# RWKV-7 products in one written order, with the memory projection's ten tiles computed whole at nine places of it

## The reference, cut to what matters

```
def step(s, inp):                                   # RWKV-7, one token, 8 heads of 64
    r_t, w_t, k_t, v_t, kk_t, a_t = inp
    sa = einsum('bhvk,bhk->bhv', s, -kk_t)
    s = s * w_t + sa[..., None] * (kk_t * a_t) + v_t[..., None] * k_t
    return s, einsum('bhvk,bhk->bhv', s, r_t)
s_final, ys = lax.scan(step, s0, xs)
m = mean(y, axis=-1); var = mean(square(y - m), axis=-1)
y = (y - m) * rsqrt(var + GN_EPS) * ln_w + ln_b
out = (y + bonus) * g

mk, mv = split(rmsnorm(mem, g_mem) @ w_mem_kv, 2)   # (256, 1024) each, used by the cross-attention
```

## Time and profile before

| | us |
|---|---|
| median of 3 runs (1435.22 to 1437.1) | 1437.06 |
| the profiled execution's own time | 1435.98 |
| its span | 1434.2 |
| PE busy in it | 1367.2 |
| RWKV jobs, from the fillers of the first to the start of `w_out` | 182.7 to 325.6 |
| experts | from 495 |

### The profile page before, as it was taken

The page is one execution under the profiler, slowest core; times in us unless marked ns, Lnnn a source line. Parts: engine busy times, 40 slices in busy tenths (PEclk is TensorE's granted clock), DMA queues, the critical chain, the costliest instruction groups (busy, mean ns, idle before and its releaser), DMA issues.

```text
span 1434.2 us, 21169 instructions
## 1 busy us (share of the span) xinstructions
PE 1367.2 (95%) x8649; PEld 689.7 (48%) x8649; DVE 440.5 (31%) x880; ACT 259.9 (18%) x487; POOL 57.5 (4%) x111
## 2 busy tenths in 40 slices
PE   8989999989999999999999899999898999988997
PEld 5667788766665533434334334333343333433342
DVE  5998845433121411221131112111131112211112
ACT  4253521204131220201101101011021010110102
POOL 4362000000000000000000000000000000000000
PEclk9999999999999999999999999999999999999999
DMA  8971311026769499999999999999999999999994
GB/s 330 201 124 59 118 66 33 32 61 255 305 241 404 159 391 378 418 430 426 427 429 428 428 428 428 428 429 429 428 428 428 429 428 429 427 428 427 427 425 172
DMA packets 43335, 471.84 MB, mean 329 GB/s; under 512 B 4992, under 2 KB 10368, under 8 KB 11520
## 3 DMA queue, kind: packets, MB, share of 16 engines
q1 hardware_dynamic: 37264, 461.42, 77.7%
q10 hardware_dynamic: 6000, 9.41, 3.4%
HBM read 465.33 MB, written 5.48 MB: 328 GB/s over the span
## 4 chain that ended last, share of the span: by engine, by line
PE 72%; DMA 21%; DVE 3%; issue 2%; ACT 1%; ACTq 1%; SPq 0%; DVEq 0%
DMA big<-in_w_gu 18%; PE bank L1189 17%; PE bank L1238 15%; PE bank L716 9%; PE bank L1112 5%; PE bank L979 2%; PE bank L799 2%; PE bank L1302 2%; PE bank L1258 2%; DMA big<-u_windows 2%; PE bank L898 1%; PE bank L1119 1%; PE bank L1214 1%; PE bank L1287 1%; PE bank L890 1%
## 5 line engine op out<-in xcount | busy, mean ns | idle before, releaser
L1189 PE MATMUL bank<-big 128*64 128x512 f32 x1920 | 428.0, 603 | 27.5 <-DMA big<-in_w_gu 27.4
L1189 PEld LDWEIGHTS bank<-big 128*64 128x64 f32 x1920 | 143.4, 138 | 309.0 <-issue 298.7
L1238 PE MATMUL bank<-big 128*64 128x512 f32 x960 | 209.4, 594 | 0.0
L716 PE MATMUL bank<-big 128*128 128x320 f32 (+1 forms) x688 | 187.6, 429 | 2.2 <-ACT big L1524 1.3
L716 PEld LDWEIGHTS bank<-big 128*128 128x128 f32 x688 | 129.5, 191 | 56.7 <-issue 6.4
L2242 DVE TENSOR_TENSOR big<-big,bank 128x320 f32<-128x320 f32 x120 | 58.6, 488 | 303.1 <-PE bank L1258 297.8
L2228 DVE TENSOR_SCALAR big<-bank 128x512 f32<-128x512 f32 x32 | 22.2, 693 | 391.9 <-PE bank L1189 361.7
L1238 PEld LDWEIGHTS bank<-big 128*64 128x64 f32 x960 | 69.9, 137 | 128.2 <-issue 126.5
L1593 ACT ACTIVATE big<-big 128x512 f32<-128x512 f32 x30 | 18.8, 626 | 448.8 <-DVE big L2228 448.7
L1353 ACT ACTIVATE big<-bank 128x320 f32<-128x320 f32 (+3 forms) x122 | 53.1, 436 | 217.8 <-PE bank L890 40.1
L1112 PE MATMUL bank<-big 128*128 128x512 f32 x192 | 85.4, 593 | 1.4 <-DVE big L2176 1.4
(11 more groups left out here) (408 smaller groups left out, 1149.1 us busy)
## 6 DMA issues: line engine op xcount, KB each, us to landing
big<-in_w_gu SPq DMA_DIRECT2D x128, 2048.0 KB, 25.1
big<-in_w_down SPq DMA_DIRECT2D x62, 2048.0 KB, 22.3
big<-in_dense SPq DMA_DIRECT2D x47, 1024.0 KB, 8.9
big<-u_windows ACTq DMA_DIRECT2D x32, 160.0 KB, 12.5
big<-in_w_down SPq DMA_DIRECT2D x4, 1024.0 KB, 20.3
big<-in_smw SPq DMA_DIRECT2D x1, 1408.0 KB, 19.4
big<-in_xT SPq DMA_DIRECT2D x2, 640.0 KB, 4.5
big<-in_consts SPq DMA_DIRECT2D x1, 1028.5 KB, 14.5
```

What stands on the lines that cost most here:

```text
L716: last = mm(b[:, 0:n], w[:, k, :], src[:, k, :], start=(k == 0), stop=(k == kt - 1))
L1189: last = mm(ps[n][part, :], xte[:, 2 * j + k, part], w[s][:, k, n * 512:n * 512 + 512], start=False, stop=end)
L1238: last = mm(ps[bank][part, :], actT[:, 4 * d + i, part], w[s][:, i, h * 512:h * 512 + 512], start=(d == 0 and i == 0), stop=end)
```

## The change

`_RATES`, `_fill`, `FILL_AT` and `FILL_DONE` go. A string `RWKV_ORDER` names all jobs of PE, the memory's tiles among them, and PE and ACT both walk through it. Each job is a small function. What moves:

- The ten memory tiles are computed whole (`mem_fill`, 8 matmuls on end), at nine places: `mk6` and `mk7` together ahead of `y0_3`, `mv00` ahead of `y2_0`, `mv01` ahead of `y3_2`, `mv10` ahead of `y4_1`, `mv11` ahead of `y5_1`, `mv20` ahead of `hh3`, `mv21` ahead of `m_0`, `mv30` between `u_1` and `m_1`, `mv31` between `u_2` and `m_2`.
- `me0` to `me3` stand ahead of `sf0` to `sf3` on PE, and L2090's work (now L2085) ahead of the additions to `m0` on DVE.
- DVE makes a mask of `v` (`vm`) in each state step, behind `m_c`'s work, and only the four of `U` (`um`) after the last; both have four places now, so none waits for an `sf`.
- ACT waits for `s5_gated` ahead of its first RWKV copy, not behind the sixteen `t` copies; its stores of the states and of the memory stand behind the exponentials.
- `m_0` waits by itself for the copies of `tk` and `tb`; the banks of `me` and `va` come from the same six.

```diff
-_RATES = (("tb0", KT), ("t", 0.32), ("gb", 0.4), ("gk", 0.4), ("y0_0", 4), ("y0", 0.6), ("y1", 0.6), ("dt1", 0.5), ("dx1", 0.5),
...
+RWKV_ORDER = ("tb0 tv0 tk0 ta0 tb1 tv1 tk1 ta1 tb2 tv2 tk2 ta2 tb3 tv3 tk3 ta3 gb4 gk4 gb0 gk0 gb1 gk1 gb2 gk2 gb3 gk3 y0_0 y0_1 y0_2 "
+              "mk6 mk7 y0_3 y1_0 y1_1 y1_2 y1_3 dt1_0 dx1_0 dt1_1 dx1_1 dt1_2 dx1_2 dt1_3 dx1_3 mv00 y2_0 y2_1 y2_2 y2_3 dt2_0 dx2_0 "
...
+              "m_2 yy2a yy2b u_3 m_3 yy3a yy3b ys0 ys1 ys2 ys3 me0 me1 me2 me3 sf0 sf1 sf2 sf3 va0 va1 va2 va3 ").split()
...
             def start_job(job):
-                for filler, k in FILL_AT.get(job, ()):
-                    fill(filler, k)
                 bank, n = JOB[job]
...
+            def mem_fill(job):
+                b = start_job(job)
...
+                    for k in range(KT):
+                        last = mm(b[:, 0:256], memT[:, k, t * P:(t + 1) * P], w[:, k, :], start=(k == 0), stop=(k == KT - 1))
+                end_job(last, job)
...
+            def state_step(job, c):
                 if c:
+                    stored(pe, f"u_{c}")
+                else:
+                    pe.wait_ge(S("u_first"), 1)
                     for i in TILES4:
+                        stored(pe, f"tk{i}")
+                        stored(pe, f"tb{i}")
...
-        um, vm = (view(at, 2, NB // 2 * HN) for at in (RW[0], RW[17]))
+        um, vm = ([view(at, 2, NB // 2 * HN) for at in ats] for ats in ((RW[0], RW[2]), (RW[17], RW[12])))
...
                 else:
                     step.read_out(tt(M[:, 0], b, scale, mul), "m_0")
+                own_tokens(vT, vm, c)
             step(tt(U[:, :, PC], own[:, :, 0], H[:, :, PC], add), "u_sample")
             for i in TILES4:
-                if i >= 2:
-                    computed(dve, f"sf{i - 2}1")
-                for src, dst, signal in ((U, um, None), (vT, vm, "uv_masked")):
...
+                own_tokens(U, um, i, "uv_masked")
+            for i in TILES4:
+                b = computed(dve, f"me{i}")
+                step.read_out(stt(YT[:, i, :], b[:, 0:T], -1.0 / HN, YT[:, i, :], mul, add), f"me{i}")
             for i in TILES4:
                 for q in range(2):
```

More of the change, by code:

```diff
@@ L193 @@
 GRAM_ORDER = (4, 0, 1, 2, 3)
-def rwkv_names():
[L198 to L223, removed]
+RWKV_ORDER = ("tb0 tv0 tk0 ta0 tb1 tv1 tk1 ta1 tb2 tv2 tk2 ta2 tb3 tv3 tk3 ta3 gb4 gk4 gb0 gk0 gb1 gk1 gb2 gk2 gb3 gk3 y0_0 y0_1 y0_2 "
[4 rows of a table added]
+              "m_2 yy2a yy2b u_3 m_3 yy3a yy3b ys0 ys1 ys2 ys3 me0 me1 me2 me3 sf0 sf1 sf2 sf3 va0 va1 va2 va3 ").split()
+MEM_V = [f"mv{q}{t}" for q in range(4) for t in range(2)]
+MEM_FILL = ["mk6", "mk7"] + MEM_V
+def rwkv_names():
+    for job in RWKV_ORDER:
+        if job.startswith("yy"):
+            if job.endswith("a"):
+                yield job[:3]
+        elif job.startswith("sf"):
+            yield from [f"{job}{q}" for q in range(2)]
+        elif job not in MEM_FILL:
+            yield job
 def job_names():
@@ new lines, in turned_over, with gram @@
+            def turned_over(job, src, i):
+                per_chunk(job, i, NC, src, lambda h, c: con("ident64")[h, :])
+            def gram(job, src, i):
+                b = start_job(job)
+                for n in range(4):
+                    t, c = (i, n) if i < 4 else (n, PC)
+                    for _, h in halves:
+                        last = mm(b[h, n * P:(n + 1) * P], src[h, t, c, :],
+                                  ar[h, t, c, :, :].rearrange("p a b -> p (a b)"), start=True, stop=True)
+                end_job(last, job)
@@ L942, in _, with chunk_out @@
                         last = mm(b[h, i * HN:(i + 1) * HN], bT[h, i, c, :], U[h, i, c, :], start=False, stop=True)
[L943 to L945 removed]
+                end_job(last, job)
+            def chunk_out(c, half):
+                b = ps[JOB[f"yy{c}"][0]] if half else start_job(f"yy{c}")
+                for i in (2 * half, 2 * half + 1):
                     for _, h in halves:
@@ L950, in _, with samples_out @@
                             last = mm(b[h, i * CH:(i + 1) * CH], M[h, c - 1, i, :], ar[h, i, c, 1, :], start=False, stop=True)
-                end_job(last, f"yy{c}")
-            for i in TILES4:
+                if half:
+                    end_job(last, f"yy{c}")
+            def samples_out(job, i):
                 pe.wait_ge(S("u_sample"), 1)
-                b = start_job(f"ys{i}")
+                b = start_job(job)
                 for _, h in halves:
@@ L958, in _, with samples_step @@
                     last = mm(b[h, 0:CH], own[h, i, 1, :], con("ident64")[h, :], start=False, stop=True)
-                end_job(last, f"ys{i}")
-            for i in TILES4:
+                end_job(last, job)
+            def samples_step(i):
                 pe.wait_ge(S("uv_masked"), i + 1)
@@ L1473, in _ @@
             act.dma_start(o["shift"], shift).then_inc(S("stores"), 16)
-            reached = [0]
-            def fillers(job=None):
-                while reached[0] < len(RWKV_JOBS) and (job is None or reached[0] <= RWKV_JOBS.index(job)):
-                    for f in FILL_DONE[RWKV_JOBS[reached[0]]]:
-                        dst = mkT[:, int(f[2]), :] if f.startswith("mk") else mv[:, int(f[3]), int(f[2]) * 256:int(f[2]) * 256 + 256]
-                        copy(dst, f, lambda b: b[:, 0:256])
-                    reached[0] += 1
+            act.wait_ge(S("s5_gated"), CT)
```

252 lines of the change are left out of this document (115 added, 137 removed), and 3 rows, old and new, of the table RWKV_ORDER.

## The result

The changed kernel took 1425.74 us (median of 4 runs, 1424.06 to 1427.28) against 1437.08 before: a ratio of 0.9923, 95% interval 0.9905 to 0.9940, so 11.3 us faster. Predicted were 1415.0 and a range of 1410 to 1425; the time lies 0.7 us outside it. Run again with six executions it took 1422.88 against 1436.15 (0.9908, 0.9892 to 0.9924), which is inside the range. The profiled execution took 1424.06, 11.9 less than the one before.

What follows compares the result with a forecast made beforehand. PE's own work was taken as the bound up to w_out: 27.5 us of switches and waits fall to 6.0, and the 21.5 gain carries whole from 1435.98 (median 1437.08) to 1414.5 (1415.6); predicted 1415.0, range 1410 to 1425.

Steps and rivals of the forecast that it cites:

- the ledger: PE's time that is no matmul, up to w_out: 27.5 us before, 6.0 after, a gain of 21.5.
- The ledger before: switches 20.1: Up to w_out in the old kernel: 55 filler groups at 0.35 us and four at 0.20 make 20.1 us.
- nine groups, 3.2: After the change nine groups of memory fillers remain, costing 3.2 us in switches.
- Waits and tail: PE's waits: before, 1.8 us for u_first, 2.4 at state readings, 3.2 from sf0 to w_out; after, 2.8 in all.
- Start. No wait, with 0.3 to spare.: First RWKV jobs: ACT's copy frees the first bank at 186.1, PE needs it at 186.4; at worst 0.5 us lost.
- The levels: Levels, y jobs: whole tiles give DVE 3.6 us each, so only y1_3 is late, by 0.2 us.
- The experts' own length as it was, 939 us.: Expected sign in the changed profile: the expert stage keeps its 939 us, its first product coming 21 us earlier.
- an expert stage that is longer: Sign that the prediction is wrong: the expert stage grows by what the mixer won.
- 1 (DVE takes part back): Levels and end: DVE late by 1 us a level and 2 at the end; gain 14.5, time 1422; 12%.
- 2 (the clock): Narrow products without fillers: PE's clock falls to half, adding 27 us against 21.5 won; 1441; 7%.
- 3 (the gain does not reach the end): Experts' stream is bound by memory and starts when it did; time 1436, within 0.2%; 5%.
- 4 (0.45 a group): Switches cost more than the rows say, 0.45 us for each filler group; time 1409; 6%.

Runs made afterwards that it cites:

- `mk7` late: Changed kernel with memory tile mk7 moved from ahead of y0_3 to ahead of mv00; RWKV's stretch took 129.67 us.
- the changed order at offset 169: Changed kernel, order unaltered, with the last experts' instructions beginning at 169 modulo 256; RWKV's stretch took 128.68 us.
- the old tail: Changed kernel with whole memory tiles but states before means and all masks after u_sample, as before; 1421.82 us, stretch 131.93.

## Why the prediction was right and wrong

It was right in direction and mechanism: the switches were the largest cost, and what PE won ahead of `w_out` was carried to the experts whole (16.9 us of it still stand at 1172 us, as at the start of `w_out`; the rest is the late start upstream). It was wrong by 10.7 us. Of that, 2.8 are in the ledger and 5.2 to 5.5 are a mechanism that it did not have; without the second block behind the loop the changed kernel takes 1417.54 and 1419.04. The rest, 2.4 to 2.7, is of the size by which sets of runs of one kernel differ (1425.74 and 1422.88 for this one).

- **"The ledger before: switches 20.1", "nine groups, 3.2."** Predicted 16.9 for 50 groups, measured 0.318 a group, 15.9. Mis-sized by 1.0, inside the stated ends of 0.30 and 0.38. One support that the prediction names is none: the 420 ns of the earlier trace rows are the length of one record, and a filler is two records that overlap, so they say nothing on 0.43 a filler. The price rests on the start-to-start rows alone.
- **Waits and tail.** The prediction had 3.4 for `u_first` and the `u` waits less `u_3`, 1.4 net for the tail and 0.2 against it for `y1_3`: 4.6. The stretch gave 18.7 in the repeat, which with 15.9 for switches and the two losses below leaves 5.0. `y1_3` showed no wait, `u_3` waited 0.59 (0.8 predicted), `ys0` 0.46 (0.6), `me0` 0.58 (0.6), and `w_out` 0.32 (not predicted). From `m_0` to `w_out` I had 31.2 us, and it took 308.65 - 277.41 = 31.24.
- **"Start. No wait, with 0.3 to spare."** This failed. I looked for the wait at the seventh job and for ACT; it was at the first one and for DVE: `tb0` takes the bank of `bo3`, which the filler tile `mk6` had covered. 3.06 us from the bo sums to `tb0` instead of 2.15 to the first filler: 0.9 lost.
- **The levels.** DVE was never late there, as computed. But 1.2 to 2.2 us were lost to the stall at 219 us, of which nothing stood in the ledger.
- These are 1.0 + 0.9 + 1.3 less 0.4 for the waits, 2.8: 18.7 instead of 21.5.
- **"The experts' own length as it was, 939 us."** This is the step that failed: it was longer by 5.2 us (5.5 in the repeat), and that decided the result. The term of the sum that was missing is the second block of instructions behind the loop, for which PE stood idle 10.78 us instead of 5.61. The prediction named "an expert stage that is longer" as a sign that it was wrong, but had no rival for it. What lay in view was the row of 5.61 us without a releaser in the profile before; I had not asked what it was, since the code there is not changed. Its address is.
- **Rivals.** 1 (DVE takes part back) did not happen in the levels. 2 (the clock) did not happen in the profile of the changed kernel nor in its repeat: 1.00 throughout, also in the 20 us of narrow products from 184.3 to 204.3, where the rule of the Trainium skill that I had weighed ("TensorE: Matmul & The Clock Gate", Part 4) would have had to bring it down if it reached such products; the trace does not bear that out. It is not far off, though: three other traces show half clock behind idle times among small products, after 0.78 twice (`mk7` late), after 2.15 (the changed order at offset 169) and after 0.83, 0.32 and 2.49 (the old tail), at a cost of 1.5 to 2.1 us each. 3 (the gain does not reach the end) did not happen. 4 (0.45 a group) is refuted by 0.318.

## What to carry to other kernels

Small products of another shape between the main ones cost 0.32 us a group here, beyond their own time, and the profile books it as busy; but whole tiles leave waits bare that scattered ones covered, so look up for each moved tile what it stood in front of (`tb0`, `va0`), and put waits behind fillers, not ahead of them. Where a program leaves a long loop while its weight stream fills the DMA engines, idle time with no releaser can be instruction fetch: an edit that adds or takes away instructions ahead of it can change its size, here between 5.1 and 11.1 us, more than many a tuning step, so compare the idle time in that place before judging an edit by its total. A change in code address can be tried for nothing, with instructions in a branch that is never taken.

## What the runs showed of the hardware

- PE's instructions came in packets of 16 KB on a queue of their own, 51 or 52 in a run. The offsets of all runs behind the loop fit blocks of 256 instructions, a fp32 matmul counted as four. Each packet moved in 0.9 to 1.4 us, but behind weight traffic at 410 to 442 GB/s two in a row were some 6 us apart, and the second was usable 5.39 to 5.50 us after the first product in all three runs that showed it apart.
- A stall of 1.2 to 2.2 us also appeared in straight code, at one fixed instruction, where 138 narrow records ran in 4 us beside transfers at 320 GB/s. It left when the transfers were moved. It ended 1.2 to 1.5 us behind the landing of a 16 KB packet.
- The clock stayed at 1.00 over 20 us of 64-row products with PE busy 19.3 of them. It went to 0.50 behind two idle times of 0.78 us in another order, and behind one of 2.15 us in one run but not in another.
